# A one-core Trainium2 kernel: where the final norm of a mixture-of-experts layer is computed and stored

## The reference

```python
def rmsnorm(x, g):
    xf = x.astype(jnp.float32)
    y = xf * lax.rsqrt(jnp.mean(xf * xf, axis=-1, keepdims=True) + EPS)
    return (y * g.astype(jnp.float32)).astype(x.dtype)

def expert_choice_ffn(h, w_router, w_gate, w_up, w_down):
    cap = EC_FACTOR * xt.shape[0] // N_EXPERTS          # 128 latent rows, 32 context rows
    affin = jax.nn.softmax((xt @ w_router).astype(jnp.float32), axis=-1)
    gates, idx = lax.top_k(affin.T, cap)
    xs = xt[idx]
    hid = jax.nn.silu(xs @ w_gate) * (xs @ w_up)        # per expert
    y = (hid @ w_down) * gates[..., None]
    out = jnp.zeros_like(xt).at[idx.reshape(-1)].add(y.reshape(-1, shp[-1]))

    xp = xp + g2 * expert_choice_ffn(h, ...)            # the same for xs
y_prompt = rmsnorm(xp, norm_final)
y_sample = rmsnorm(xs, norm_final)
```

## Time and profile before

| | us |
|---|---|
| timed runs | 3546.9, 3543.01, 3539.9 (median 3543.01) |
| the profiled execution: its own time | 3545.69 |
| the profiled execution: its span | 3543.9 |
| DVE has the last expert's outputs ready (`y_p`) | at 3468.5 |
| last expert's scatter landed | at 3479.4 |
| last output tile issued for storing | at 3534.1 |

### The profile page before, as it was taken

The page is one execution under the profiler, slowest core; times in us unless marked ns, Lnnn a source line. Parts: engine busy times, 40 slices in busy tenths (PEclk is TensorE's granted clock), DMA queues, the critical chain, the costliest instruction groups (busy, mean ns, idle before and its releaser), DMA issues.

```text
span 3543.9 us, 52567 instructions
## 1 busy us (share of the span) xinstructions
PE 3301.7 (93%) x21172; PEld 3005.3 (85%) x21172; DVE 2142.5 (60%) x2376; ACT 1757.5 (50%) x1820; POOL 587.7 (17%) x611
## 2 busy tenths in 40 slices
PE   6899999998999999998959999999999999999991
PEld 4677777777788877886759999999999999999991
DVE  5544444354442354235967777777777777777774
ACT  5553543454452255224345555555565555556552
POOL 1046136102321022401010000000000000000001
PEclk8999999998899999998979999999999999999995
DMA  7676465577214421443567898888889888888976
GB/s 262 235 257 223 165 230 196 200 255 257 81 49 137 170 75 33 161 154 126 192 220 246 263 287 277 277 270 262 258 265 284 278 268 278 266 258 267 279 232 263
DMA packets 544951, 775.87 MB, mean 219 GB/s; under 512 B 16160, under 2 KB 409600, under 8 KB 536144
## 3 DMA queue, kind: packets, MB, share of 16 engines
q1 hardware_dynamic: 507072, 616.60, 53.2%
q0 software_dynamic: 37776, 157.84, 13.7%
HBM read 708.19 MB, written 66.19 MB: 219 GB/s over the span
## 4 chain that ended last, share of the span: by engine, by line
PE 80%; DVE 5%; DMA 5%; ACT 4%; POOL 3%; issue 3%; ACTq 0%; POOLq 0%; DVEq 0%
PE PS L843 32%; PE PS L845 13%; PE PS L620 12%; PE PS L791 11%; PE PS L737 2%; PE PS L716 2%; DVE wlo L1200 1%; DMA arena_ab<-k_rope 1%; PE PS L566 1%; PE PS L567 1%; PE PS L660 1%; ACT whi L917 1%; PE PS L725 1%; PE PS L755 1%; PE PS L825 1%
## 5 line engine op out<-in xcount | busy, mean ns | idle before, releaser
L843 PE MATMUL PS<-xT,hi_f 128*128 128x320 f32 x4096 | 1056.9, 346 | 0.0
L1513 DVE TENSOR_TENSOR lo_f<-raw_f,hi_f 128x2048 fp32r<-128x2048 f32 x384 | 879.0, 2289 | 272.6 <-ACT hi_f L1124 272.0
L845 PE MATMUL PS<-xT,lo_f 128*128 128x160 f32 x4096 | 965.8, 236 | 0.0
L1200 DVE TENSOR_TENSOR wlo<-raw,whi 128x2048 fp32r<-128x2048 f32 x204 | 473.3, 2336 | 639.6 <-ACT whi L917 639.0
L1124 ACT ACTIVATE hi_f<-raw_f 128x2048 fp32r<-128x2048 f32 x384 | 734.0, 1911 | 176.9 <-PE PS L845 87.5
L845 PEld LDWEIGHTS PS<-xT,lo_f 128*128 128x128 f32 x4096 | 782.1, 191 | 0.0
L843 PEld LDWEIGHTS PS<-xT,hi_f 128*128 128x128 f32 x4096 | 768.6, 188 | 0.0
L917 ACT ACTIVATE whi<-raw 128x2048 fp32r<-128x2048 f32 x204 | 387.3, 1915 | 574.2 <-PE PS L791 303.8
L843 PE MATMUL PS<-hid,hi_f 128*128 128x320 f32 x2048 | 533.9, 346 | 0.0
L845 PE MATMUL PS<-hid,lo_f 128*128 128x160 f32 x2048 | 482.9, 236 | 0.0
L845 PEld LDWEIGHTS PS<-hid,lo_f 128*128 128x128 f32 x2048 | 390.7, 191 | 0.0
(11 more groups left out here) (268 smaller groups left out, 4621.5 us busy)
## 6 DMA issues: line engine op xcount, KB each, us to landing
raw_f<-w_gate SPq DMA_DIRECT2D x128, 1024.0 KB, 6.1
raw_f<-w_up SPq DMA_DIRECT2D x128, 1024.0 KB, 5.8
raw_f<-w_down SPq DMA_DIRECT2D x128, 1024.0 KB, 5.4
raw<-w_ada SPq DMA_DIRECT2D x96, 1024.0 KB, 5.2
raw<-w_in SPq DMA_DIRECT2D x60, 1024.0 KB, 5.3
raw<-w_out SPq DMA_DIRECT2D x48, 1024.0 KB, 5.4
arena_ab<-x_sample POOLq DMA_DIRECT2D x8, 1024.0 KB, 12.5
arena_cd<-x_sample POOLq DMA_DIRECT2D x8, 1024.0 KB, 6.4
```

The source lines that it names most:

```text
L843: nc.tensor.matmul(PS[:, b + m, 0:2 * CAP], hi_f[:, n % NSPL_F, r, w], x, start=(kt == 0), stop=False, skip_group_check=True)
L845: ins = nc.tensor.matmul(PS[:, b + m, 0:CAP], lo_f[:, n % NSPL_F, r, w], x[:, 0:CAP], start=False, stop=(kt == last_kt), skip_group_check= ...
L1200: nc.vector.tensor_tensor(wlos[slot(n)], raws[slot(n)], whis[slot(n)].bitcast(F32), ALU.subtract).then_inc(lo_ok, 1)
L1513: nc.vector.tensor_tensor(lo_f[:, n % NSPL_F], raw_f[:, n % NRAW_F], hi_f[:, n % NSPL_F].bitcast(F32), ALU.subtract).then_inc(f_lo_ok, 1)
```

## The change

The last expert (e = 15) is taken out of the loops and written out on its own (`more` is false). In it

- nothing is gathered, modulated, taken or turned for a following expert;
- POOL first lands the scatter of expert 14, then loads the ten residual tiles one after the other, to wherever memory is free: three at once (the buffers of the modulation tables and of the gathered rows), two more when the first two have been stored again, two when the gate and up pieces are used (over `xT`), three into `raw_f` slots after pieces 20, 21 and 22. The constants `nf_s`, `nf_p` and `fold` are loaded before, within expert 14;
- ACT squares tile 2p after piece `PAIR_AT[p]` and tile 2p+1 one piece later, then takes the two roots; DVE forms the two reciprocal roots and multiplies, two and three pieces later; POOL stores.

These tiles lack the last expert's contribution. That expert's own rows are read once more (an indirect gather of `resid_s` and `resid_p` into `gr_s` and `gr_p`), its outputs are added to them on chip, squared, summed (the four column parts of a context row are summed by one matmul with `fold`), normalised, and written over their rows in `y_sample` and `y_prompt` by an indirect store without addition, after all ten tile stores have landed. `fin` and its separate stage are gone.

```diff
+PAIR_AT = (7, 14, 16, 18, 20)
...
                         for lag in range(2):
+                            if pair_step(n, lag) is not None:
+                                tile_square(2 * pair_step(n, lag) + lag)
+                        if pair_step(n, 2) is not None:
+                            tile_root(pair_step(n, 2))
...
+            def tile_square(i):
+                act.wait_ge(f_in[i], 16)
+                if i:
+                    act.wait_ge(f_sq, i)
+                nc.scalar.activation(junk3, tiles[i], ACT.Square, accum_out=fs[:, 4, i:i + 1]).then_inc(f_sq, 1)
...
-                    if n in (4, 6, 8, 10, 12):
+                    if more and n in (4, 6, 8, 10, 12):
                         modulate(n // 2 - 2, e * 16 + 32, e * 5 + 5)
...
+                    if not more:
+                        if pair_step(n, 2) is not None:
+                            tile_rstd(pair_step(n, 2))
+                            tile_norm(2 * pair_step(n, 2))
+                        if pair_step(n, 3) is not None and n < PIECES_E - 1:
+                            tile_norm(2 * pair_step(n, 3) + 1)
+                        if n == PIECES_E - 2:
+                            tile_norm(TT - 1)
...
+            nc.vector.tensor_tensor(y_p[:], y_p[:], gr_p, ALU.add).then_inc(e_add, 1)
+            for c in range(4):
+                s = slice(c * CC, (c + 1) * CC)
+                nc.vector.tensor_tensor(y_s[:, s], y_s[:, s], gr_s[:, s], ALU.add).then_inc(e_add, 1)
...
+            scatter(NE - 2)
...
+            for i in range(3):
+                load_tile(i)
+            store_tile(0)
+            store_tile(1)
+            for i in range(2):
+                pool.wait_ge(f_out[i], 16)
+                load_tile(3 + i)
+            pool.wait_ge(f_used, (NE - 1) * PIECES_E + 16)
+            load_tile(5)
+            load_tile(6)
+            raw_free(20)
+            load_tile(7)
+            store_tile(2)
...
+            for i in range(TT):
+                pool.wait_ge(f_out[i], 16)
+            pool.wait_ge(ic_ok, NE)
+            pool.wait_ge(e_ok, 2)
+            nc.gpsimd.indirect_dma_start(out=ys, out_offset=bass.IndirectOffsetOnAxis(ap=ic_s[:, 0:1], axis=0),
+                                         in_=y_s[:], in_offset=None).then_inc(s_out, 16)
```

More of the change, by code:

```diff
@@ L835, in _, with expert @@
                 turn_tokens(j)
-            with pe.Fori(0, NE) as e:
+            def expert(e, more):
                 def ktile(b, n, r, x, kt, last_kt):
@@ L895, in _ @@
                         turn_outputs(2, e)
-                    pe.wait_ge(h_in, e * 5 + 7 + cc)
-                    pe.wait_ge(x_lo, e * 4 + 4 + cc)
-                    turn_tokens(cc)
+                    if more:
+                        pe.wait_ge(h_in, e * 5 + 7 + cc)
+                        pe.wait_ge(x_lo, e * 4 + 4 + cc)
+                        turn_tokens(cc)
                     if cc in (1, 2):
                         turn_outputs(cc - 1, e)
-            turn_outputs(3, NE - 1)
+                if not more:
+                    turn_outputs(3, e)
+            with pe.Fori(0, NE - 1) as e:
+                expert(e, True)
+            expert(NE - 1, False)
+            pe.wait_ge(nf_in, 16 * (2 + Q))
+            pe.wait_ge(e_sq, 1)
+            nc.tensor.matmul(PS[:, 0, 0:1], fold[:], esq[:, 4:5], start=True, stop=True).then_inc(e_fold, 1)
         @block.scalar
@@ L1171, in _ @@
             expert_hi(NE - 1, False)
[L1174 to L1182, removed]
+            act.wait_ge(f_sq, TT)
+            act.wait_ge(e_add, 1)
+            nc.scalar.activation(junk3[:, 0:DQ], y_p[:], ACT.Square, accum_out=esq[:, 4:5]).then_inc(e_sq, 1)
+            for c in range(4):
+                act.wait_ge(e_add, c + 2)
+                act.wait_ge(e_sq, c + 1)
+                nc.scalar.activation(junk3[:, 0:CC], y_s[:, c * CC:(c + 1) * CC], ACT.Square,
+                                     accum_out=esq[:, c:c + 1]).then_inc(e_sq, 1)
+            act.wait_ge(e_ms, 1)
+            nc.scalar.activation(es[:, 1, :], es[:, 0, :], ACT.Sqrt).then_inc(e_root, 1)
         @block.vector
@@ L1530, in _ @@
             dve.wait_ge(tab_in, 16 * (3 + 3 * Q))
[L1531 removed]
+            link(nc.vector.scalar_tensor_tensor(out=a2_p, in0=a2_p, scalar=1.0, in1=y_p[:], op0=ALU.add, op1=ALU.mult))
             link(nc.vector.scalar_tensor_tensor(out=a2_s[:], in0=a2_s[:], scalar=1.0, in1=y_s[:], op0=ALU.add, op1=ALU.mult))
@@ L1916, in _ @@
-            for z in range(NF):
-                pool.wait_ge(f_out[z], 16 * ((TT - z + NF - 1) // NF))
+            dma(nf_s[:], t["norm_final"].partition_broadcast(P)).then_inc(nf_in, 16)
+            for m in range(Q):
+                dma(nf_p[m * CAP_P:(m + 1) * CAP_P, :],
+                    t["norm_final"][m * DQ:(m + 1) * DQ].partition_broadcast(CAP_P)).then_inc(nf_in, 16)
+            dma(fold[:], t["k_fold"]).then_inc(nf_in, 16)
+            pool.wait_ge(ig_ok, NE)
+            pool.wait_ge(x_tr, NE * 4)
```

153 lines of the change are left out of this document (105 added, 48 removed).

## The result

| us | before | after |
|---|---|---|
| median of the timed runs (lowest to highest, number) | 3541.45 (3536.9 to 3546.9, 4) | 3511.33 (3508.78 to 3513.4, 4) |
| profiled execution: time, span | 3545.69, 3543.9 | 3510.94, 3509.1 |

The ratio is 0.9914, with a 95% interval of 0.9903 to 0.9926: about 30 us faster. The forecast was 3513.4, in a range of 3500 to 3528.

A forecast was written before the change was run, and what follows sets the result against it. It took the experts to be bound by TensorE and the tail by transfers. A shorter tail, −51.8, and a later y_p, +22.2, gave −29.6 us; from the median 3543.0 that made 3513.4, range 3500 to 3528.

The forecast's parts named there:

- The new tail: From y_p ready to the end: 9.4 arithmetic, 0.9 issue, 8.3 indirect stores, 5.0 end; 23.6 us against 75.4.
- What goes: Last expert's unused turns and xT step go, so y_p could be ready at about 3466.0 instead of 3468.5.
- The DMA engines: Last expert: tiles go ahead of weights, nine transfers of 2.5 us before piece 19, which lands at 3442.7.
- The signs that I had named: Profile checks: DMA step wrong if splits of pieces 18, 19 start before 3437; DVE step if outside 38 to 50.
- ACT's order: Piece 19's split precedes square 3 and piece 16's eviction in ACT's list: 1.9 + 1.9 + 0.4, to 3446.9.
- DVE's work: From the sums of piece 16 to y_p: 41.3 us of work and about 2.5 of waits, 43.8.
- Tiles 0 and 1 cost DVE nothing: On DVE in the last expert, two products, 4.7, and one pair of roots replace 7.2 us of modulate.
- Constants in expert 14: Loading 1.38 MB (3.3 us) behind expert 14's scatter, taken at 0, bound 1.
- The table loads: Three on ACT in the last expert; a page's drain of about 1.4 us per switch was left out of the sum.
- (a): Rival: weights hardly held up in the last expert, tile traffic sharing evenly; 3502.5 us, chance 0.2 (3501 to 3507).
- (b): Rival: dearer tile transfers, 3518, and a lower TensorE clock after stops, up to 3526; chance 0.2 (3519 to 3528).
- (c): Rival: loads of tiles 5 to 9 set the pace through ACT's squares; kernel slower, 3551 at 15.5 us each; chance 0.03.

The follow-up runs named there:

- e4: Kernel before without the last expert's unused gather, modulate steps and turns, its separate last stage kept: 3544.74 us, ratio 1.0009.
- e6: Changed kernel with the loads of tiles 5 and 6 issued after the split of piece 19: 3510.29 us, ratio 0.9916.
- e1: Changed kernel with tile loads and stores cut to 64 of 2048 columns, tiles 5 to 9 in other buffers: 3505.64 us, ratio 0.9897.
- e8: Changed kernel with filler matmuls on TensorE ahead of piece 14, piece 19 and the last turns: 3508.07 us, ratio 0.9905.
- e7: As e6, and tile 1 is loaded after the split of piece 8, tile 2 after that of piece 11: 3506.59 us, ratio 0.9904.
- e10: As e7, with the last tile's product later, y_p's product and store before y_s's, stores 2 and 3 behind the second gather: 3506.71 us, ratio 0.9903.

## Why the prediction was right

The time was right to 2 us and the kernel's gain to half a microsecond (30.1 measured, 29.6 forecast). The large parts of the mechanism held: the tail shrinks by over 50 us, tile transfers go ahead of weights, and DVE's list sets the pace behind piece 16. The step from the transfers to the sums of piece 16 did not hold, and some terms were off and made up for each other.

- **The new tail**, 23.6: 21.6. The arithmetic was 9.55 (9.4 said) and POOL's issue 0.8 (0.9). The term that was mis-sized is the indirect stores, 5.4 from first issue to last landing instead of 8.3: they land like plain stores (4.8 in the earlier trace rows), 4.6 and 4.1 behind their issues, and the second is issued 1.3 behind the first. The end behind the landing took 5.8 instead of 5.0.
- **What goes**, `y_p` 2.5 earlier: 1.7 by e4.
- **The DMA engines**, piece 19 at 3442.7 in before's times: its split came at 3435.2, which is 3438.8 there. The order of the queues held (87 to 15). Two things failed. First, the count of nine transfers ahead of piece 19: loads 5 and 6 are issued at 3432.7, at 3433 to 3437 POOL's queue has still only 41% of the time, and they fall on piece 20. With seven transfers the same sum gives 3437.7. Second, and more, the path: the sums of piece 16 are late by piece 11 and not by piece 19. I had a stall of 1 to 2 us at piece 9, yet that piece came earlier than before (its split 18.6 us behind the beginning against 22.1). ACT waited 6.9 for piece 11, which became a stop of TensorE of 3.7 us and a slow clock worth 2.7. With before's distance from the eviction after piece 15 to the sums of piece 16 (6.2 us) that alone gives 64.6 + 6.2 = 70.8 of the 71.7, and e6, where piece 19 isn't waited for, has 71.1. That the sum with seven transfers would give much the same (70.5) is luck.
- **The signs that I had named.** The splits of pieces 18 and 19 were not to start before 3437. Piece 18's starts at 3428.35, or 3431.9 in before's times, and waits for TensorE and not for a weight; by that sign the DMA step is wrong, as it is by the path. (The sign was badly put: I had expected piece 18 at 3435 myself.)
- **ACT's order**: from piece 19's split to the eviction, 1.9 + 1.9 + 0.4, as said. But little of the delay hangs on it: the list costs the sums of piece 16 at most 0.9 us in after.
- **DVE's work**, 43.8 from sums 16: 48.0, of which 38.0 busy and 9.3 waiting (6.2 for piece 20, 1.7 for roots, 1.4 for turns). I had 41.3 and 2.5. The work was counted by the durations of single rows, which add up to 40.9 in after too, yet on DVE a long row's successor begins some 0.08 us before its recorded end (3486.09 + 0.75 against 3486.75), which over the 59 rows takes 2.9 us off; the waits lacked the late piece, which stood in the wrong step. The stretch was inside the bounds that I had set, 38 to 50.
- **Tiles 0 and 1 cost DVE nothing**: by themselves, yes, since e1, with full products, has the sums of piece 16 at 64.2. But they stand behind the late split of piece 11 and ahead of `usum` and `hraw`, so that the lateness reaches TensorE as a stop of 3.7 us before piece 14. Both products are on the chain that leads from piece 11's landing to the issue of piece 20's load. I had looked for stops before pieces 17 to 19 only.
- **Constants in expert 14**, 0: TensorE has no wait there in after.
- **The table loads**: 1.28, and the root's ACTIVATE begins at its end (3448.22 + 1.28, 3449.51). The 1.4 us of drain that the Trainium skill counts (ScalarE: Activation LUTs, "What ACT_TABLE_LOAD costs") is in no row here, and the sum was right to leave it out.
- **Rivals.** (a), even sharing: the share in time was as uneven as the earlier trace rows. (b), lower clock: the clock fell as it said, to 0.50 behind each stop, which is what the Trainium skill warns of (TensorE: Matmul & The Clock Gate, "Why this matters for your kernels"). It costs TensorE 2.7 us at the first stop, where I had none; that it costs the kernel nothing is shown by e8 only together with the other order of the transfers, and behind the second stop it is untested. (c), the loads of tiles 5 to 9: ACT waited for none of them in after, they landed 5.7 to 10.7 us behind their issues.

The DMA term was 3.8 too long and the DVE term 4.2 too short. That the two cancelled is not all luck: piece 20's wait, which is in the DVE term, is what loads 5 and 6 cost when they don't fall on piece 19, and e8, where they do, has the same `y_p` to 0.2 us, with 77.4 and 42.5 close to the 75.5 and 43.8 of the forecast. But the 7.5 us in the first length came by a way that the forecast did not have, and that they were of the size it gave to another way is luck.

## What to carry to other kernels

Work that is moved under a bound engine is not free because the engine that takes it is half idle: of the 54 us that the shorter tail gave, 24 went back, to transfers (7.5 or more), products (10.3), squares (4.2) and 2.1 that transfers and products share. Such prices are had one by one by making one kind of the moved work small and leaving its instructions in place. Before a transfer is put beside a stream of weights, compare packet sizes: in these traces the queue with the larger packets took the larger share. And look for the first piece that is late, not only for the one just ahead of the stage: here one late piece early in the expert delayed the load of another nine pieces on, by the slot that it needed. A different time of issue (e6, e7, e10) mostly chose which piece was late, and gave a few microseconds at best.

## What was not expected of the hardware

- Two DMA queues with work for the same engines sent nearly equal numbers of packets (190 to 196, 190 to 202, 364 to 401), so shares in time went from 87 to 15 at 7.5 against 1.0 KB to 72 to 32 at 2.7 against 1.0 KB.
- The last expert began at 3357.6 to 3371.4 us in thirteen profiled executions of kernels that are nearly alike up to there. The end of a kernel changed only at its end is therefore better measured from a point just ahead of the change.
